# Gate rows of the first block: one turn, a DRAM row and broadcast reads in place of 32 PE turns

## The reference

```python
mod = c_act @ w_ada[l] + b_ada[l]
sh1, sc1, gt1, sh2, sc2, gt2 = jnp.split(mod, N_MOD, axis=-1)
...
y = jnp.concatenate([y_lru, y_pool], axis=-1) @ w_out[l]
x = x + gt1[:, None, :] * y
h = modulate(rmsnorm(x, g_norm_ffn[l]), sh2, sc2)
f = (jax.nn.silu(h @ w_ffn_gate[l]) * (h @ w_ffn_up[l])) @ w_ffn_down[l]
x = x + gt2[:, None, :] * f
```

## Time and profile before

| | |
|---|---|
| Median of 3 runs | 2579.7 us (2579.15 to 2582.84) |
| The profiled execution | 2581.12 us, span of the core 2579.4 us |
| PE busy | 2537.2 us, 98% of the span |
| DVE, ACT, POOL busy | 1584.5, 1270.1 and 78.7 us |
| Mean granted clock of PE | 0.997 of full speed |
| HBM read | 549.99 MB, 214 GB/s over the span |

### The profile page before, as it was taken

How to read it: one execution, slowest core, us unless ns; L and a number is a source line. 1 busy time by engine, 2 the same in 40 slices (tenths; PEclk the granted TensorE clock), 3 DMA queues, 4 the chain that set the end, 5 groups by cost and what they waited for, 6 DMA issues and landing times.

```text
span 2579.4 us, 32511 instructions
## 1 busy us (share of the span) xinstructions
PE 2537.2 (98%) x12421; PEld 2069.7 (80%) x12421; DVE 1584.5 (61%) x1937; ACT 1270.1 (49%) x1674; POOL 78.7 (3%) x165
## 2 busy tenths in 40 slices
PE   7999999999999999999999999999999999999999
PEld 1688878888888888888877788888888888888887
DVE  1467997764455455566787687556666666644445
ACT  2354454444444444454577656445555555544463
POOL 0012110100000000000000000000000000000000
PEclk9999999999999999999999999999999999999999
DMA  9999888865555555565544655555555555555564
GB/s 384 383 378 368 335 323 275 297 218 194 182 194 188 174 191 184 192 206 180 163 128 127 194 173 180 185 191 181 194 179 188 186 184 183 183 192 185 186 229 130
DMA packets 351340, 553.67 MB, mean 215 GB/s; under 512 B 18656, under 2 KB 200944, under 8 KB 350464
## 3 DMA queue, kind: packets, MB, share of 16 engines
q1 hardware_dynamic: 331616, 480.83, 55.7%
q0 software_dynamic: 19616, 71.34, 7.4%
HBM read 549.99 MB, written 2.13 MB: 214 GB/s over the span
## 4 chain that ended last, share of the span: by engine, by line
PE 92%; DMA 3%; DVE 2%; ACT 1%; issue 1%; SPq 0%; DVEq 0%; ACTq 0%
PE pair L1365 27%; PE pair L1367 27%; PE pair L1366 27%; DMA mod_raw<-in_w_ada 2%; PE pair L1347 1%; PE pair L1349 1%; PE pair L1348 1%; PE misc L1505 1%; PE pair L1966 1%; DVE w_lo L2043 1%; PE misc L1381 1%; PE misc L1909 1%; DMA raw<-in_w_in 0%; PE misc L1747 0%; ACT w_hi L712 0%
## 5 line engine op out<-in xcount | busy, mean ns | idle before, releaser
L2043 DVE TENSOR_TENSOR w_lo<-raw,w_hi 128x1024 fp32r<-128x1024 f32 x848 | 1018.0, 1204 | 849.1 <-ACT w_hi L712 846.7
L712 ACT ACTIVATE w_hi<-raw 128x1024 fp32r<-128x1024 f32 x848 | 882.2, 1043 | 1016.9 <-PE pair L1367 935.2
L1365 PE MATMUL pair<-w_hi,a_hi 128*128 128x512 f32 x2048 | 808.8, 395 | 3.5 <-DVE a_lo L2151 2.5
L1367 PE MATMUL pair<-w_hi,a_lo 128*128 128x512 f32 x2048 | 799.1, 390 | 0.0
L1366 PE MATMUL pair<-w_lo,a_hi 128*128 128x512 f32 x2048 | 798.2, 390 | 0.0
L1365 PEld LDWEIGHTS pair<-w_hi,a_hi 128*128 128x128 f32 x2048 | 385.2, 188 | 84.9 <-issue 4.4
L1367 PEld LDWEIGHTS pair<-w_hi,a_lo 128*128 128x128 f32 x2048 | 385.0, 188 | 81.5
L1366 PEld LDWEIGHTS pair<-w_lo,a_hi 128*128 128x128 f32 x2048 | 385.4, 188 | 77.7 <-issue 0.5
L1365 PE MATMUL pair<-w_hi,hid_hi 128*128 128x512 f32 x704 | 275.0, 391 | 0.0
L1367 PE MATMUL pair<-w_hi,hid_lo 128*128 128x512 f32 x704 | 274.0, 389 | 0.0
L1366 PE MATMUL pair<-w_lo,hid_hi 128*128 128x512 f32 x704 | 273.9, 389 | 0.0
(11 more groups left out here) (388 smaller groups left out, 2155.1 us busy)
## 6 DMA issues: line engine op xcount, KB each, us to landing
raw<-in_w_in SPq DMA_DIRECT2D x88, 1024.0 KB, 5.3
raw<-in_w_up SPq DMA_DIRECT2D x176, 512.0 KB, 4.3
raw<-in_w_out SPq DMA_DIRECT2D x48, 1024.0 KB, 5.1
raw<-in_w_ffn_gate SPq DMA_DIRECT2D x88, 512.0 KB, 3.6
raw<-in_w_ffn_up SPq DMA_DIRECT2D x88, 512.0 KB, 4.6
mod_raw<-in_w_ada POOLq DMA_DIRECT2D x86, 512.0 KB, 6.9
raw<-in_w_ffn_down SPq DMA_DIRECT2D x32, 1024.0 KB, 5.0
raw<-in_w_down SPq DMA_DIRECT2D x32, 1024.0 KB, 5.1
```

The costliest lines, as they stand in the source:

```text
L712: run(w_hi[:, h % HALF_SLOTS, 0:n, :], raw[:, h // 2 % RAW_SLOTS, at0:at0 + n, :], ACT.Copy).then_inc(hi_ready, 1)
L1365: pe.matmul(o, hi[:, own], w_hi[:, slot, kk, :], start=(h == kk == 0), stop=False)
L1367: mm = pe.matmul(o, lo[:, own], w_hi[:, slot, kk, :], start=False, stop=(h == ph.halves - 1 and kk == n - 1))
L2043: dve.tensor_tensor(w_lo[:, slot, 0:n, :], raw[:, h // 2 % RAW_SLOTS, at0:at0 + n, :], w_hi[:, slot, 0:n, :].bitcast(F32), ALU.subtract).t ...
```

## The change

The gate vector is turned once: `gate_turn` turns the 16 columns of `mod` into 16 rows of 128 numbers. ACT copies the 16 rows to a corner of `gt` (`gate_out`), stores them by its own queue as one row of 2048 numbers in a DRAM scratch tensor (`gate_store`), and for each block reads 512 numbers of that row back over all 128 partitions (`gate_load`, a transfer of 256 KB into `gt`). For the second vector the same follows in `down1`.

In `w_out` the turn stands after half 2 of block 0, copy and store at place 3, the read for block 0 at place 5, and that for a later block at place 1, once DVE's multiply of the block before is done. In `down1` the turn stands after half 0, copy and store at place 3, and the reads at the same places as in `w_out`. PE's waits for the copies go; PE waits once, at half 6 of block 0 of `w_out`, for the store.

```diff
+        gate_rows = nc.dram_tensor("gate_rows", [2, D], F32, kind="Internal").ap()
...
-        GT2_AT, GT1_ROWS, TURNED1_AT, GT1_AT = 1, 5, 3, 6
+        TURNED1_AT, GATE_OUT, GATE_LOAD, GATE_NEXT = 3, 3, 5, 1
...
-            def gate_row(n):
-                act.wait_ge(gt_row, n + 1)
-                if n:
-                    act.wait_ge(res_ready, n)
-                run(gt[:], misc[:, 0 if n < XB else 2, :], ACT.Copy).then_inc(row_ready, 1)
+            def gate_out(i, bank):
+                act.wait_ge(gt_row, i + 1)
+                if i:
+                    act.wait_ge(res_ready, XB)
+                done(run(gt[0:KC, 0:P], misc[0:KC, bank, 0:P], ACT.Copy))
+            def gate_store(i):
+                done.wait()
+                act.dma_start(by_chunk(gate_rows[i]), gt[0:KC, 0:P]).then_inc(row_ready, 16)
+            def gate_load(n):
+                if n % XB == 0:
+                    act.wait_ge(row_ready, gate_stored(n // XB))
+                else:
+                    act.wait_ge(res_ready, n)
+                act.dma_start(gt[:], gate_rows[n // XB:n // XB + 1, n % XB * COLS:(n % XB + 1) * COLS].to_broadcast([P, COLS])).then_inc(row_ready, 16)
...
-            def gate_row(a, b, bank):
-                for m in range(4):
-                    mm = pe.transpose(misc[:, bank, m * P:(m + 1) * P], mod[:, a * KC + 4 * b + m:a * KC + 4 * b + m + 1].to_broadcast([P, P]), ident[:])
-                mm.then_inc(gt_row, 1)
+            def gate_turn(a, bank):
+                pe.transpose(misc[0:KC, bank, 0:P], mod[:, a * KC:(a + 1) * KC], ident[:]).then_inc(gt_row, 1)
...
-                    if h == 2 and b:
-                        pe.wait_ge(row_ready, b)
+                    if (b, h) == (0, 6):
+                        pe.wait_ge(row_ready, gate_stored(0))
                     mods_beside(IN_PLACES + b * w_out.halves + h - MOD_LAG)
-                    if h == GT1_ROWS:
-                        if b:
-                            pe.wait_ge(n_f, XB + b)
-                        else:
-                            pe.wait_ge(mod_ready, 6)
-                        gate_row(2, b, 0)
+                    if h == 2 and b == 0:
+                        pe.wait_ge(mod_ready, 6)
+                        gate_turn(2, 2)
```

More of the change, by code:

```diff
@@ L185, in spread_landing, with gate_stored, gate_landed @@
         return mod_landing(len(mod_seq) + n)
+    def gate_stored(n):
+        return 16 * (5 * n + 1)
+    def gate_landed(n):
+        return 16 * (n + n // 4 + 2)
     def mod_used_by(a, k):
@@ L998, in beside_w_out @@
                     norm_turned(1, b - 1)
-                elif n == GT1_AT:
-                    gate_row(b)
+                if b == 0 and n == GATE_OUT:
+                    gate_out(0, 2)
+                    gate_store(0)
+                elif n == (GATE_NEXT if b else GATE_LOAD):
+                    gate_load(b)
             def sums_w_out(b, c):
@@ L1028, in beside_down1 @@
                     hidden_high(up1.blocks, 1)
-                if place == (GT2_AT if b else LAST_HIDDEN + 1):
-                    gate_row(XB + b)
+                if b == 0 and place == GATE_OUT:
+                    gate_out(1, 2)
+                    gate_store(1)
+                elif place == (GATE_NEXT if b else GATE_LOAD):
+                    gate_load(XB + b)
             stream(down1, None, w_in2, beside=beside_down1)
@@ L1406, in beside @@
                         other(h)
-                    if n == 2 and h == 0:
-                        gt2_rows(b)
                     if h == 2 and b:
@@ L1431, in normed_yet @@
                 return before
-            def gate_row(a, b, bank):
-                for m in range(4):
-                    mm = pe.transpose(misc[:, bank, m * P:(m + 1) * P], mod[:, a * KC + 4 * b + m:a * KC + 4 * b + m + 1].to_broadcast([P, P]), ident[:])
-                mm.then_inc(gt_row, 1)
-            def gt2_rows(b):
-                pe.wait_ge(mod_ready, 10)
-                if b:
-                    pe.wait_ge(row_ready, XB + b)
-                gate_row(5, b, 2)
+            def gate_turn(a, bank):
+                pe.transpose(misc[0:KC, bank, 0:P], mod[:, a * KC:(a + 1) * KC], ident[:]).then_inc(gt_row, 1)
             pe.wait_ge(consts, 1)
@@ L1697, in last_hidden_turned @@
                 if h == 0:
-                    gt2_rows(0)
+                    pe.wait_ge(mod_ready, 10)
+                    gate_turn(5, 2)
                 elif h == LAST_HIDDEN:
@@ L2434, in add_gated @@
                 cols = slice(b * COLS, (b + 1) * COLS)
-                dve.wait_ge(row_ready, n + 1)
+                dve.wait_ge(row_ready, gate_landed(n))
                 dve.tensor_tensor(pair[:, c], pair[:, c], gt[:, None, :].to_broadcast([P, T, COLS]), ALU.mult).then_inc(res_ready, 1)
@@ L2442, in add_halves @@
                 cols = slice(b * COLS, (b + 1) * COLS)
-                dve.wait_ge(row_ready, b + 1)
+                dve.wait_ge(row_ready, gate_landed(b))
                 for t in range(T):
```

## The result

The changed kernel takes 2587.28 us (median of 15 runs, 2585.5 to 2590.86) against 2581.59 us (2579.15 to 2587.32) for the kernel before in the same comparison: ratio 1.0022, 95% interval 1.0015 to 1.0030, so 5.7 us slower. The prediction was 2580.5 us, +0.8 us, with 2584.5 as its upper end. The profiled executions stand at 2586.42 us (span 2584.7) and 2581.12 us (span 2579.4), 5.3 us apart.

The account below looks back on a forecast made before the run. PE was taken to bound `down1`; in `w_out` PE, DVE and DMA were full, a transfer setting its end. -1.6 (`down1`) + 0 (PE in `w_out`) + 2.4 (transfers) = +0.8 us, so 2580.5 us; range 2576.0 to 2584.5.

Parts of the forecast that it names:

- At 400 GB/s, 1.05 MB take 2.6 us: `w_out`: four new reads delay the tile ACT waits for at 363.14 by 2.1 to 2.6 us, taken as 2.4.
- the bound of 5.1: `w_out`: upper bound in us for the four reads, from broadcasts of 512 KB that took up to 10.3 us to land.
- later by as much: End of `w_out`: DVE's last split comes about 2.4 us later, and the first matmul of `up1` by as much.
- The term of -1.6: `down1`: 16 turns go and one comes, 15 x 0.11 = 1.65 us, all of it arriving at the end.
- PE alone sets the pace: `down1`: PE busy for 199.75 of 200 us, DVE 107.50, ACT 96.61, DMA share 0.58, so only PE bounds the phase.
- The price of a turn, 0.11 us: PE in both phases: each turn costs 0.11 us, with nothing fixed for a group.
- PE's turns buy nothing in `w_out`: `w_out`: PE gains 0 to 0.5 us, counted as 0, since DVE is not free for `add_halves` before `up1`'s splits.
- the 1 us foreseen: `w_out`: PE would have short waits for `w_lo`, some 1 us in sum, first in blocks 2 and 3.
- DVE has no idle time at `add_gated`: `w_out`: expected sign in the changed profile, no idle time of DVE at `add_gated`.
- the reads are hidden: Rival, `w_out`: ACT's queue gets its share without holding back the tile of 363.1; -2.0 us, 2577.7; chance 0.30.
- PE is the pace everywhere: Rival, both phases: all time taken off PE counts; -3.3 us, 2576.4; chance 0.10.
- the first gate row comes late: Rival, `w_out` block 0: read lands over 13 us after issue, delaying DVE's multiply; 1.5 us at 14.5, say 2586; chance 0.07.

Follow-up runs that it names:

- e3: Kernel before with the change in `down1` only, `w_out` left as before: 2582.81 us, ratio 1.0001.
- e1: Kernel before with all turns and copies kept, plus four unused reads of 256 KB on ACT's queue in `w_out`: 2589.84 us, ratio 1.0028 to the kernel before.
- e5: Changed kernel with only block 0's read in `w_out`, those of blocks 1 to 3 left out: 2585.20 us, ratio 1.0009 to the kernel before.
- e9: Kernel before, turns kept, plus one read of 256 KB on ACT's queue at half 5 of `w_out`'s block 0: 2584.05 us, ratio 1.0005.
- e10: Kernel before, turns kept, plus one read of 256 KB on ACT's queue at half 1 of `w_out`'s block 3: 2583.07 us, ratio 1.0001.
- e11: Kernel before, turns kept, plus four reads of 16 columns on ACT's queue in `w_out`, at the changed kernel's places: 2582.26 us, ratio 0.9997.
- e13: Kernel before, turns kept, plus eight reads of 256 KB on ACT's queue in `w_out`, two in each block: 2589.25 us, ratio 1.0030.
- e4: Changed kernel with `w_out`'s reads for blocks 1 to 3 cut to 128 columns: 2586.68 us, ratio 1.0018 to the kernel before.
- e2: Kernel before with the change in `w_out` only, `down1` left as before: 2588.29 us, ratio 1.0021.
- e6: Changed kernel with `up1`'s third split moved behind `add_halves`: 2582.22 us, ratio 1.0003 to the kernel before.
- e12: Changed kernel with `up1`'s third split behind `add_halves` and `down1`'s turn of x after half 3 instead of 2: 2580.58 us, ratio 0.9994 to the kernel before.
- e8: Kernel before with `up1`'s third split moved behind `add_halves`: 2582.64 us, ratio 1.0003.
- e7: Kernel before with the change in `down1` only, its turn of x after half 3 instead of 2: 2580.46 us, ratio 0.9992.

## Why the prediction was wrong

**What a byte more costs in a full phase.** The step that failed is "At 400 GB/s, 1.05 MB take 2.6 us", taken as 2.4: it measured 5.5, above even the bound of 5.1 that I had set aside. Transfers by ring in the same stretch of 78 us (285 to 363 us), packets, MB and share; q0 is POOL's, q1 SP's, q10 ACT's. Before:

```profile
DMA packets 12871, 30.49 MB, mean 391 GB/s; under 512 B 769, under 2 KB 3583, under 8 KB 12866
...
q0 software_dynamic: 4690, 17.05, 55.9%
q1 hardware_dynamic: 8176, 13.37, 47.0%
```

After:

```profile
DMA packets 12670, 30.41 MB, mean 390 GB/s; under 512 B 795, under 2 KB 2989, under 8 KB 12665
...
q0 software_dynamic: 4555, 16.57, 54.3%
q1 hardware_dynamic: 7534, 12.73, 44.2%
q10 hardware_dynamic: 576, 1.05, 4.5%
```

The sum is the same, so the reads were not hidden and the engines did not lose rate. As the stretch cuts the two kernels at other points of `w_out`, each ring's bytes are counted here from `w_out`'s first matmul, for 26 and for 94 us. The trace records sixteen landings for each tile; the eighth and the last of the second tile are in the right columns:

| MB moved | SP at 26 us | POOL at 94 | SP at 94 | ACT at 94 | tile's 8th landing, us | its last, us |
|---|---|---|---|---|---|---|
| before | 2.59 | 19.54 | 14.48 | 0 | 88.41 | 93.38 |
| e3 no reads here | 2.67 | 19.58 | 14.56 | 0 | 87.67 | 91.64 |
| after | 2.35 | 19.27 | 13.62 | 1.06 | 94.78 | 98.88 |
| e1 reads alone | 2.34 | 19.31 | 13.64 | 1.05 | 94.70 | 99.13 |
| e5 one read | 2.32 | 19.51 | 14.15 | 0.27 | 91.36 | 97.09 |
| e9 first read alone | 2.33 | 19.50 | 14.17 | 0.26 | 91.34 | 93.96 |
| e10 last read alone | 2.66 | 19.52 | 14.33 | 0.26 | 90.03 | 96.21 |
| e11 tiny reads | 2.38 | 19.52 | 14.24 | 0.03 | 91.03 | 93.90 |
| e13 doubled reads | 2.37 | 18.62 | 13.48 | 1.88 | 97.14 | 101.53 |

POOL's ring is fed at the pace at which DVE uses its tiles, and from 42 to 94 us it kept 0.22 MB/us, before and after. SP's weight ring gets what is left: in the same time it went from 5.03 to 13.62 MB after, 0.165 MB/us. At 94 us the changed kernel's SP ring was 0.86 MB short, for 1.06 MB of reads and store, and 0.86 MB at 0.165 MB/us are 5.2 us: the second tile is 5.5 us later. My divisor was the rate of all rings together, which would be right if all of them fell behind alike; the tile that counts was on the one that fell behind most.

That is an account of the bytes, made after the fact, and not a law. First, part of what SP loses does not go by bytes. In every kernel with a read at half 5 of block 0, where the transfers start again after a quiet stretch, SP's ring stands at 2.32 to 2.38 MB after 26 us, against 2.59 to 2.78 without one; e11, whose read there is of 8 KB, has the same loss and keeps it to 94 us, where it is 0.24 to 0.32 MB short of the kernels without reads. e10, with its read at the end, has none at 26 us. Why a small read costs that much there was not found. Second, the second megabyte was borne by others: from e1 to e13 ACT's ring moved 0.83 MB more by 94 us, POOL's 0.69 less and SP's 0.16 less, which at 0.165 MB/us would be 1.0 us where the tile came 2.4 later. Why POOL's ring then gives was not tried; a likely reason is that DVE, late for lack of weights, asks for its modulation tiles later. Nor was any run made with the same reads on SP's or POOL's own queue, so what the third queue itself adds is open.

The Trainium skill, page "DMA: Bandwidth & Descriptors", section "Queues, rings and completion order", has each DMA engine go round the queues that have work, a packet at a time. The traces agree in the outcome, the small new queue being served beside the full one, gate rows landing after 4.0 to 8.2 us and the weights 0.86 MB short; no record here shows the order of packets on one engine.

What stays open is the size of the one-read runs. In e5 and e9 the three rings had moved the same bytes within 0.02 MB at 94 us, and the second tile landed at 97.09 and 93.96. The difference is in the last of its parts: the eighth of the sixteen landed at 91.36 and 91.34, the fourteenth at 92.44 and 93.69, the last two at 95.58 and 97.09 in e5 and at 93.70 and 93.96 in e9. A tile counts as there when its slowest part is, so single parts are worth up to 3 us, and what decides them was not found. By the eighth landing the runs are in order: 87.67 to 88.59 with no reads, 90.0 to 91.4 with tiny ones or one, 93.3 to 94.8 with four, 97.1 with eight (e4, with its narrow ones, 91.7). The last landings of the kernels with the four full reads (after, e1, e2, e6, e12) agree within 0.6 us.

**What stands behind the late tile.** The sum had nothing for the norm chain, +1.24 us. The prediction let the first matmul of `up1` come "later by as much" as the split. But PE had nothing to do ahead of the chain for 5.7 us and came back at 1.2 GHz. e10 and e1 have the same 8.66 us of chain with the late split; e6 and e9, where `add_halves` hardly waits, have 7.66 and 7.40. The +0.47 us of `up1` behind it goes with how many of its first matmuls still run at the lower clock, 14 instead of 12, but e3 and e8 have 14 as well and no late tile.

**`down1`.** The term of -1.6 measured -0.36. "PE alone sets the pace" was read from windows, with DVE busy for 107.50 of 200 us. That was true for every instruction but the turns of x, three places where PE met DVE with nothing to spare (0.15 us between DVE's end and PE's start, the handover itself), and where I took 0.44 us away ahead of them. The price of a turn, 0.11 us, was right: e7 gives 1.72 us for 15 turns.

**What held.** That PE's turns buy nothing in `w_out`: without them PE's last matmul came at 94.49 us in e4 and e5, 0.73 earlier than before, and `add_halves` did not follow; in the changed kernel it came no earlier at all (95.59 us against 95.22), since PE waited 1.3 us more for DVE, about the 1 us foreseen. All of these have reads; no run leaves out both the turns and the reads. Further held that the transfers are the new cost and the third split the place where it comes out, that DVE has no idle time at `add_gated`, and that the store and reads are cheap for ACT (0.33 us an issue) and in time for their users. The gate row's instructions after, 270 to 372 us, ns min/median/max:

```profile
L1014 ACTq DMA_DIRECT2D gt<-gate_rows x4: 326/327/353, 284.4 to 347.9; - x4
L2450 DVE TENSOR_TENSOR pair<-pair,gt x3: 1223/1223/1224, 298.2 to 346.7; 128x1024 f32<-128x1024 f32 x3
...
DMA to landing us min/median/max: 4.0/7.0/8.2
```

Of the rivals, "the reads are hidden" and "PE is the pace everywhere" would both have made the kernel faster; e1 rules out the first, and e3, with 0.36 us of 1.65 in `down1`, the second; "the first gate row comes late" did not happen, as the first read was issued at 284.4, landed in 8.2 us at most, and DVE needed it at 298.2. By terms: -1.6 was -0.4, 2.4 was 5.5, 0 for the norm chain was 1.2, and with 0.5 of scatter in `up1` 0.8 forecast became 6.8. The spans show 5.3 of it, since this execution happened to start `w_out` 1.5 us earlier.

## What to carry to other kernels

When the DMA engines are full, do not price new bytes by the whole rate alone: find out which queue is paced by its user and which gets what is left, for here the latter fell 0.86 MB short for 1.06 MB added, and the tile on it came 5.5 us later where the whole rate gives 2.6. Then look at who waits for the last tile, and what stands behind that wait: taking the split out of the way gave the 5 us back, though the tile was as late as ever. Before counting a gain on the bound engine, look at each cross-engine wait in the phase and how narrowly it is met, not at the mean load of the others: work that looks like pure cost may be what hides a wait. Moving the waiting instruction by one step gave all of it back.

## What the runs showed of the hardware

- The sixteen transfer engines, at some 400 GB/s, kept that sum (390 against 391 GB/s) with a third queue added; the split between queues changed, not the sum.
- The last landing of a tile can differ by 3 us between two profiled executions whose queues have moved the same bytes (97.09 against 93.96) and whose eighth landings agree (91.36 and 91.34), and by 1.7 us between kernels alike in that phase (91.64 against 93.38).
- Four reads of 64 bytes to each partition, 0.03 MB in all, moved `add_halves` by 0.5 us and the whole by nothing measurable (0.9997), but the eighth landing of the second tile by 2.4 us at least (91.03 against 87.67 to 88.59).
- Behind nearly the same idle time of PE the granted clock fell once and once not: 0.54 after 1.97 us (e12), 1.00 after 1.80 us (e6).
